# Expert weights in rows of 16 KB and 2 MB transfers, and 32-column products for the first layer's latent tokens

## What is computed

```python
def expert_choice_ffn(h, w_router, w_gate, w_up, w_down):
    cap = max(1, EC_CAPACITY * t // N_EXPERTS)
    aff = jax.nn.softmax((h @ w_router).astype(F32), axis=-1)
    gate, idx = lax.top_k(jnp.swapaxes(aff, 1, 2), cap)
    xs = jax.vmap(lambda hb, ib: hb[ib])(h, idx)
    hid = jax.nn.silu(jnp.einsum('becd,edf->becf', xs, w_gate)) * jnp.einsum('becd,edf->becf', xs, w_up)
    y = jnp.einsum('becf,efd->becd', hid, w_down) * gate[..., None].astype(h.dtype)
...
```

## Time and profile before

| | us |
|---|---|
| median of 3 runs | 2789.28 |
| lowest and highest of the runs | 2784.68, 2790.75 |
| the profiled execution | 2783.82 |
| its span in the trace | 2781.6 |
| PE busy in the span | 2236.2 (80%) |
| DVE, ACT, POOL busy | 716.8, 407.9, 209.8 |
| mean granted TensorE clock | 0.899 of full speed |
| DMA traffic | 564.11 MB, mean 203 GB/s |

### The profile page before, as it was taken

How to read it: one execution, slowest core, us unless ns; L and a number is a source line. 1 busy time by engine, 2 the same in 40 slices (tenths; PEclk the granted TensorE clock), 3 DMA queues, 4 the chain that set the end, 5 groups by cost and what they waited for, 6 DMA issues and landing times.

```text
span 2781.6 us, 28441 instructions
## 1 busy us (share of the span) xinstructions
PE 2236.2 (80%) x11582; PEld 1109.5 (40%) x11582; DVE 716.8 (26%) x1311; ACT 407.9 (15%) x880; POOL 209.8 (8%) x174
## 2 busy tenths in 40 slices
PE   4898999926238785999999995999899867777774
PEld 0543666616238443222222222454597422222221
DVE  0205332266756523100111101110254330000001
ACT  1013221132121111000000001100253100000001
POOL 0000000031322000001111101000000000000000
PEclk8999999956557895999999997999999879999997
DMA  8225431020111332899999993110310459999996
GB/s 315 80 91 200 131 117 50 0 85 31 61 38 54 143 133 87 343 367 361 366 367 362 383 361 131 61 53 8 114 54 25 181 231 415 414 411 414 411 416 247
DMA packets 113431, 564.11 MB, mean 203 GB/s; under 512 B 13552, under 2 KB 26352, under 8 KB 64160
## 3 DMA queue, kind: packets, MB, share of 16 engines
q1 hardware_dynamic: 101568, 522.55, 48.1%
q0 software_dynamic: 10416, 34.58, 4.5%
q10 hardware_dynamic: 1328, 5.24, 0.5%
HBM read 532.87 MB, written 29.46 MB: 202 GB/s over the span
## 4 chain that ended last, share of the span: by engine, by line
PE 66%; DMA 17%; DVE 10%; ACT 2%; issue 1%; POOL 1%; SPq 1%; DVEq 0%; ACTq 0%; POOLq 0%
PE ps L1584 17%; PE ps L1592 7%; PE ps L1377 5%; DMA work_sb<-expert_w_gate 5%; DMA work_sb<-expert_w_down 5%; DMA work_sb<-expert_w_up 4%; PE ps L452 4%; PE ps L1850 3%; PE ps L748 3%; PE ps L637 2%; PE ps L1828 2%; PE ps L1837 2%; PE ps L241 2%; PE ps L1913 2%; DMA ring_sb<-ada_w 2%; PE ps L747 1%
## 5 line engine op out<-in xcount | busy, mean ns | idle before, releaser
L1584 PE MATMUL ps<-work_sb 128*64 128x512 f32 x1536 | 370.7, 614 | 71.1 <-DMA work_sb<-expert_w_gate 31.6
L1584 PE MATMUL ps<-ring_sb,work_sb 128*64 128x512 f32 x1536 | 365.6, 609 | 57.7 <-DMA ring_sb<-expert_w_up 21.1
L1584 PEld LDWEIGHTS ps<-work_sb 128*64 128x64 f32 x1536 | 109.5, 139 | 327.7 <-issue 327.6
L1584 PEld LDWEIGHTS ps<-ring_sb,work_sb 128*64 128x64 f32 x1536 | 105.5, 138 | 301.4 <-issue 283.5
L1692 DVE TENSOR_TENSOR work_sb<-ps,work_sb 128x512 f32<-128x512 f32 x32 | 20.6, 687 | 684.9 <-PE ps L1592 356.9
L1377 PE MATMUL ps<-ring_sb,work_sb 128*128 128x512 f32 x320 | 139.6, 599 | 2.7 <-DVE work_sb L1978 1.9
L241 PE MATMUL ps<-ring_sb,sT_sb 128*32 128x512 f32 x384 | 98.9, 670 | 39.9 <-DMA ring_sb<-ada_w 39.9
L1743 POOL DMA_INDIRECT hl_rows<-work_sb x32 | 45.6, 1425 | 1013.5 <-DVE work_sb L1706 921.8
L1663 ACT ACTIVATE work_sb<-ps 128x1024 f32<-128x1024 f32 x16 | 16.4, 1024 | 642.5 <-PE ps L1592 333.7
L947 PE MATMUL ps<-work_sb 32*32 32x32 f32 x384 | 10.9, 236 | 123.7 <-DVE work_sb L1133 123.7
L452 PE MATMUL ps<-ring_sb,work_sb 128*128 128x512 f32 (+1 forms) x288 | 105.9, 530 | 0.9 <-DVE work_sb L349 0.9
(11 more groups left out here) (321 smaller groups left out, 2835.2 us busy)
## 6 DMA issues: line engine op xcount, KB each, us to landing
work_sb<-expert_w_gate SPq DMA_DIRECT2D x64, 1024.0 KB, 10.7
ring_sb<-expert_w_gate SPq DMA_DIRECT2D x64, 1024.0 KB, 11.7
ring_sb<-expert_w_up SPq DMA_DIRECT2D x64, 1024.0 KB, 13.4
work_sb<-expert_w_up SPq DMA_DIRECT2D x64, 1024.0 KB, 12.3
ring_sb<-expert_w_down SPq DMA_DIRECT2D x64, 1024.0 KB, 12.6
work_sb<-expert_w_down SPq DMA_DIRECT2D x64, 1024.0 KB, 11.9
ring_sb<-ada_w SPq DMA_DIRECT2D x96, 512.0 KB, 5.5
ring_sb<-wout SPq DMA_DIRECT2D x16, 512.0 KB, 8.9
```

The source lines that it names most:

```text
L1584: mm = pe.matmul(ps[64 * e:64 * e + 64, bank + n, :], lat_src[:, k, 64 * e:64 * e + 64], us[e][:, n * 512:(n + 1) * 512], start=(k == 0), ...
```

## The change

1. A piece of expert weights becomes 2 MB: 512 rows of one expert's matrix, four neighbouring rows to a partition (16 KB together in HBM). A product takes 4 pieces, and a piece serves four steps k. The buffer keeps its 8 MB: two pieces in the ring, two in `MORE`. `x_free` is raised every four k, and the counts that wait for it follow.
2. `paired` and `cols` use the order by fours, for all stages.
3. In the first layer the latent matmuls are 32 columns wide in place of 64: eight a step k in place of four, with the same moving operands. In the second layer they stay 64 wide.

```diff
 def paired(m):
-    return m.reshape(KT // 2, P, 2, -1).transpose(0, 2, 1, 3).reshape(D, -1)
+    return m.reshape(KT // 4, P, 4, -1).transpose(0, 2, 1, 3).reshape(D, -1)
 def cols(k):
-    return slice(256 * (k // 2) + k % 2, 256 * (k // 2) + 256, 2)
+    return slice(512 * (k // 4) + k % 4, 512 * (k // 4) + 512, 4)
 def landed(pe, u):
-    pe.wait_ge(w_land[u % RING], 16 * (u // RING + 1 + (3 * NPAIR if u >= U_MOE[0] else 0)))
+    pe.wait_ge(w_land[u % RING], 16 * (u // RING + 1 + (3 * NPAIR if u >= U_MOE[0] and u % RING < 4 else 0)))
-        MORE = region(19456, 8 * D, "p (s j n) -> p s j n", s=4, j=2)
+        MORE = region(19456, 8 * D, "p (s j n) -> p s j n", s=2, j=4)
 def place(i):
-            if i % 8 < 4:
-                return ring[:, 2 * (i % 8):2 * (i % 8) + 2, :], w_land[2 * (i % 8)]
-            return MORE[:, i % 8 - 4], w_land[2 * (i % 8) - 7]
+            if i % 4 < 2:
+                return ring[:, 4 * (i % 4):4 * (i % 4) + 4, :], w_land[i % 4]
+            return MORE[:, i % 4 - 2], w_land[i % 4]
 def used(l, p, m):
-            return 24 * (NPAIR * l + p) + 8 * m + 8
+            return 12 * (NPAIR * l + p) + 4 * m + 4
 def product(p, m, lat_src, ctx_src, bank, bank_c):
                 for k in range(KT):
                     us = []
                     for e in range(2):
-                        rows, land = place(k // 2 * 2 + e)
+                        rows, land = place(k // 4 * 2 + e)
                         pe.wait_ge(land, 16 * (u0 // RING + 3 * (NPAIR * l + p) + m + 1))
-                        us.append(rows[:, k % 2, :])
+                        us.append(rows[:, k % 4, :])
+                    wide = 32 if l == 0 else 64
                     for n in range(2):
-                        for e in range(2):
-                            mm = pe.matmul(ps[64 * e:64 * e + 64, bank + n, :], lat_src[:, k, 64 * e:64 * e + 64],
+                        for g in range(0, P, wide):
+                            e = g // 64
+                            mm = pe.matmul(ps[g:g + wide, bank + n, :], lat_src[:, k, g:g + wide],
                                            us[e][:, n * 512:(n + 1) * 512], start=(k == 0), stop=(k == KT - 1))
-                            if l == 1 and n == 1 and k % 2 == 1:
+                            if l == 1 and n == 1 and k % 4 == 3:
                                 mm.then_inc(mp["x_free"], 1)
...
-                                if n == 1 and k % 2 == 1:
+                                if n == 1 and k % 4 == 3:
                                     mm.then_inc(mp["x_free"], 1)
 def expert_rows(sp, l, p, i):
-            name = ("expert_w_gate", "expert_w_up", "expert_w_down")[i // 8]
-            src = t[name][l].rearrange("(q e) (k r j) n -> q e k r (j n)", e=2, r=P, j=2)
+            name = ("expert_w_gate", "expert_w_up", "expert_w_down")[i // 4]
+            src = t[name][l].rearrange("(q e) (k r j) n -> q e k r (j n)", e=2, r=P, j=4)
             to, land = place(i)
-            src = src[p, i % 2, i // 2 % 4, :, :].rearrange("q r n -> (q r) n")
+            src = src[p, i % 2, i // 2 % 2, :, :].rearrange("q r n -> (q r) n")
 def first_rows(sp, l, more):
-            for i in range(4 if more else 0, 8 if more else 4):
+            for i in range(2 if more else 0, 4 if more else 2):
 def moe_sync(sp, l):
-            x0 = 24 * NPAIR * l
+            x0 = 12 * NPAIR * l
             with sp.Fori(0, NPAIR - 1) as p:
-                for i in range(8, 32):
-                    sp.wait_ge(mp["x_free"], x0 + i - 7 + p * 24)
-                    expert_rows(sp, l, bass.ds(p + i // 24, 1), i % 24)
+                for i in range(4, 16):
+                    sp.wait_ge(mp["x_free"], x0 + i - 3 + p * 12)
+                    expert_rows(sp, l, bass.ds(p + i // 12, 1), i % 12)
...
```

More of the change, by code:

```diff
@@ L1765, in first_rows @@
                 sp.wait_ge(w_free, U_MOE[l])
-            for i in range(4 if more else 0, 8 if more else 4):
+            for i in range(2 if more else 0, 4 if more else 2):
                 expert_rows(sp, l, slice(0, 1), i)
         def moe_sync(sp, l):
-            x0 = 24 * NPAIR * l
+            x0 = 12 * NPAIR * l
             with sp.Fori(0, NPAIR - 1) as p:
-                for i in range(8, 32):
-                    sp.wait_ge(mp["x_free"], x0 + i - 7 + p * 24)
-                    expert_rows(sp, l, bass.ds(p + i // 24, 1), i % 24)
-            for i in range(8, 24):
-                sp.wait_ge(mp["x_free"], x0 + 24 * (NPAIR - 1) + i - 7)
+                for i in range(4, 16):
+                    sp.wait_ge(mp["x_free"], x0 + i - 3 + p * 12)
+                    expert_rows(sp, l, bass.ds(p + i // 12, 1), i % 12)
+            for i in range(4, 12):
+                sp.wait_ge(mp["x_free"], x0 + 12 * (NPAIR - 1) + i - 3)
                 expert_rows(sp, l, slice(NPAIR - 1, NPAIR), i)
@@ L2110, in _ @@
             moe_sync(sp, 0)
-            sp.wait_ge(mp["x_free"], 24 * NPAIR)
+            sp.wait_ge(mp["x_free"], 12 * NPAIR)
             stream_units(sp, U_MOE[0], len(stream))
```

## The result

| | before | changed |
|---|---|---|
| median | 2787.5 us | 2879.3 us |
| lowest and highest | 2784.7, 2790.8 | 2876.4, 2886.6 |
| profiled execution (span) | 2783.8 (2781.6) | 2876.4 (2874.1) |

The ratio is 1.033, with a 95% interval of 1.031 to 1.036: the change makes the kernel 92 us slower. The forecast was 2845 us, slower, with a range from 2772 to 2890: 55.5 us more were forecast, and 92 came.

What follows compares the result with a forecast made beforehand. First-layer expert pairs were taken as bound by PE, second-layer pairs by DMA. First layer +21, second +31, the very end +3.5: +55.5 us on a 2789.3 us median gives 2845 us, range 2772 to 2890.

Steps and rivals of the forecast that it cites:

- The mechanism: Both expert stages: the buffer acts as two halves, each half's 12.4 us turn-around looping with PE's work on it.
- A (the clock holds): Rival, both expert stages: the granted clock stays up after PE's waits; +12 us, 2801 us in total; chance 0.17.
- B (faster): Rival, first layer: gathers and scatters slip into DMA idle time, PE keeps its gain; -18 us, 2771 us; chance 0.15.
- the signs that were named: First-layer k 2.6 us, waits about 2, pair 75-77, DMA share below 0.95; second-layer clock 0.7-0.8, below 400 GB/s.
- PE's gain: First layer: a k takes 2.58 us instead of 2.86, 6.7 us a pair if the weights are there.
- Rows of 16 KB: Expert weight transfers: 1.5% of transfer time saved against 8 KB rows, so 9.80 us for 4 MB.
- the turn-around of 12.4 us: Half the buffer, 4 MB, freed until usable again: 0.14 issue, 2.3 latency, 9.80 transfer, 0.13 landing to PE.
- Gathers and scatters: First layer: two thirds of 5.7 us, 3.8 us a pair, on the path; second layer: 3.6 us a pair.
- The clock: Second layer: one fall in each half product, 1.7 us; first layer: one fall a pair, 0.8 us.
- The waits for expert weights: First layer: PE waits some 2 us in a product; pair 75.3 us before clock falls, 67.7 if PE never waited.
- my sum: Second-layer pair: 8.8 + 12.4 + 1.2 = 22.4 us a product, 67.1 us a pair.
- +21 and +34.5: First layer +21 us; second layer +31 us, with +3.5 us for four k left after the last transfer.

Runs made afterwards that it cites:

- experiment 1: Kernel before with only the first layer's latent products made 32 columns wide, pieces staying 1 MB in 8 KB rows: 2743.2 us, ratio 0.984.
- experiment 3: Kernel before with 32-column groups and 1 MB pieces in 8 KB rows, but waited for and freed four at a time: 2889.5 us, ratio 1.036.
- experiment 8: Changed kernel with expert-stage gathers (all but a layer's first) and scatters cut to 16 rows, result incomplete: 2838.8 us, ratio 1.020.
- experiment 6: Changed kernel with the second layer's second half of output columns computed for 256 of 512 (k above 0), result incomplete: 2869.7 us, ratio 1.030.
- experiment 7: Changed kernel with those second-layer columns cut to 256 of 512, plus seven unneeded matmuls behind each second-layer half: 2855.2 us, ratio 1.024.
- experiment 4: Changed kernel with four unneeded 256-column matmuls behind every four k of the second layer: 2887.9 us, ratio 1.036.
- experiment 5: Changed kernel with four unneeded matmuls only behind second-layer halves after which PE waited long (both of gate, first of down): 2893.9 us, ratio 1.038.

## Why the prediction was right, and where it was off

**The mechanism held.** The buffer as two halves, a half's turn-around in a loop with PE's work on it, is what experiments 1 and 3 isolate: 146 us between them, for granularity alone. The sign and the two places were right. Rivals A (the clock holds) and B (faster) fall with stage clocks of 0.95 and 0.87 and pairs longer than before. Of the signs that were named, the k of 2.57 us, the waits on expert DMAs, a DMA share under 0.95 in the first layer and under 400 GB/s in the second came. The first-layer pair (78.4 to 81.5 us, forecast 75 to 77), the length of the waits in it (up to 6.1 us, forecast about 2) and the second layer's clock (0.87, forecast 0.7 to 0.8) lay outside.

**PE's gain held.** 2.58 us a k was forecast, 2.57 came. The gain of the groups was forecast at 6.7 us a pair if the weights are there; experiment 1 shows 5.5 (44 / 8), since DMA then sets the pair.

**Rows of 16 KB held.** 1.5% of the transfer time was estimated. In the changed kernel two pieces issued together at a moment when nothing was being moved (DMA share 0.00 from 1408.30 to 1409.20) landed like this (the view of the issuing line, 1408 to 1409.4):

```profile
DMA to landing us min/median/max: 7.5/9.6/11.8
```

With 0.58 us between the issues, 2 MB took 11.8 + 0.58 - 7.5 = 4.9 us (forecast 4.90), and 2.6 us were no transfer (forecast 2.3; in the earlier trace rows the engines still moved 410 GB/s from 1166.40 to 1166.80, after the first issue, so that queue was not quite idle). Experiment 3 gives 10 us for the whole kernel, at the edge of the noise; 0.8 us a pair, as forecast, would be 13.

**The first term that was mis-sized is the turn-around of 12.4 us.** It is nearly right for a half that meets an idle queue. In the chain of waits of the changed kernel's second layer the lowest of the DMA steps (issue of the second piece to landing) are 11.84, against 11.5 by my terms. But of the chain's 21 steps between 2330 and 2834 us the mean is 14.3 and the highest 19.25. Over all 43 halves issued there, on the chain or not, the mean is 14.0. The forecast adds 1.2 us for gathers and scatters, so 12.7 stand against 14.0: as an estimate 1.3 us in each of a pair's three loops. The steps in part:

```profile
2384.34 13.62 DMA work_sb<-expert_w_up
...
2405.78 14.46 DMA work_sb<-expert_w_down
...
2437.99 19.25 DMA ring_sb<-expert_w_up
...
2466.35 11.84 DMA ring_sb<-expert_w_down
...
2486.16 11.84 DMA ring_sb<-expert_w_gate
```

The 19.25 belongs to the half of up that starts at 2457.38 in the timeline above. The part of the buffer before it had been freed only at 2430.3 and its transfer, for which PE waited 6.86 us, was still under way when this one was issued at 2437.4. That is the first thing I left out: I gave each loop an empty queue. Of the 43 halves only 4 were issued after the one before had landed, and these took 12.2 us on average, the other 39 14.2. My reading, which no run isolates: once one half is late (a slow clock, a gather), the two are issued close together, the second queues behind the first, and both then reach PE close together, so that DMA idles next. So one delay is paid in several halves.

**Gathers and scatters** were taken at 3.8 us a first-layer pair on the path; experiment 8 shows 3.7 (29.4 / 8). That agreement is partly luck: half of the 29 us is PE's busy time (558.5 to 543.8), at a clock of 0.97 in place of 0.95, and not a shorter path. In the second layer I took all 3.6. The cut gives 1.0 there (7.8 / 8), little more than the 1% to which stages repeat, and 2.2 in the kernel before, so 3.6 was too much even for the latter. That the long waits hold most of them in the changed kernel is a guess.

**The clock is the second mis-sized term, too high in one layer and too low in the other.** For the second layer one fall in each half product at 1.7 us was forecast: by that much the 16 records behind the wait of 2.44 us took longer in the earlier trace rows (5.35 us against 3.65), with the granted clock at 0.50 for 3.4 us. In the timeline 26 of the stage's 48 halves are slow, by 51 us together, 6.4 us a pair where six falls are 10.2. (Cut into windows of 0.5 us, the stage has 784 at a granted clock of 1.00, 252 at 0.50 and 50 between. With these two levels the mean of 0.87 is 0.26 of 543 us, 141 us at 0.50, but in part of that PE waits.) What the clock is worth is shown only in the altered form of experiments 6 and 7: 14 us for the stage, from 0.82 to 0.94. In the first layer I took one fall a pair, 0.8 us. PE is busy 558.5 us there and 528.0 in experiment 1, with the same products at a clock of 1.00: 3.8 us a pair. The waits for expert weights came near the forecast there, 8.6 us a pair (68.6 / 8) against 7.6 (75.3 - 67.7). So the first layer's excess is mostly the clock. The second layer's is waits, 16.9 us of PE's idle time a pair against about 12 in my sum (67.1 - 6 x 8.8, less 2.1 us of transposes), and there the clock term, too high, hid part of it.

The forecast had the clock fall in every half product; it fell in 26 of 48. In experiments 4 and 5 a higher clock (0.95, 0.90) did not shorten the stage by itself (544.8 and 552.2 us, against 543.0).

So the 92 us are, by stage: first layer +46.4, of which the groups are -44.2 and the coarse halves +90.6 (634.3 - 543.7); second layer +46, all from the coarse halves. Against the forecast of +21 and +34.5 the excess is 25 and 12 us.

**What stays open.** With gathers and scatters cut, a first-layer pair takes 76 us where my terms give 71.5 plus the clock. Fetches of instructions explain little of it by themselves: their queue has 39 packets in the first stage (1103.2 to 1737.5 us), and 39 too in that of experiment 1, which takes 68.5 us a pair. Whether they cost more where PE waits for every 4 MB, no run here varied. How the second stage's 46 us divide between the clock and transfers that queue behind each other isn't settled either: experiments 4 and 5 failed to part them. The split into 29 us of PE's busy and 17 us of its idle time says where the time lies, not what would be won: in experiment 6 work that was taken out came back as waits.

## What to carry to other kernels

In this kernel, which fills its buffer while it empties it, the size of the part that is given back at once mattered more than transfer efficiency. In another one of this kind compare a part's turn-around (latency, transfer, and the wait behind the other part) with the work that stands between, and do it for a part that is late, not for the idle case. Here, at 421 GB/s in the second layer and with some six 1 MB transfers queued (an estimate: 1 MB landed 15.6 us after its issue, the median of the 25 pieces issued from 2432.3 to 2495.5 us, and took 2.5 us to move), larger DMAs had some 10 us to win, and the coarser hand-over had 146 to lose. And of two edits in one change each should be timed alone: here one was worth -45 us and hid behind the other.

## What the runs showed that was not expected

Taking 22% of PE's product work out of a stage (experiment 6) gave only 13 of 543 us: the waits grew by 35 us and, with the granted clock down from 0.87 to 0.82, the slow halves by 23. Adding 3.3 us of work that nobody needs to each half (experiment 7) made the stage 14 us shorter. In the changed kernel's second stage a half was slow behind every wait from 3.23 us on and behind none up to 2.44 us; between them it went both ways.

Products of 32 columns, four side by side, ran at 2.57 us for six passes, 0.43 us a pass, the same as the 64-column ones two side by side; twice as many weight loads for the latent tokens (16 records a k in place of 8) cost nothing visible. By this comparison what had cost 0.28 us a k was alternating between 64 and 32 columns; experiment 1, which stops alternating, gets a k of 2.57 us (1339.55 to 1342.12 in its timeline).
